# Dependencies written by hand, another end of the program and another column order in a decoder layer on eight cores

## The reference

```
h  = rms_norm(x, g_pre_mix);  q, k, v, u, gates = split(h @ w_in)
q, k = rope(q), rope(k)                     # 12 heads of 64
for (window, dilation) in ((128,1), (512,4), (2048,16)):   # 4 heads each
    out_g, lse_g = causal window attention on keys t - i*dilation
o_attn = sum_g softmax_g(lse_g) * out_g     # 256 wide
y_pool = multi-scale trailing means of u, mixed per group, scaled
merged = sigmoid(gate_a) * (o_attn @ w_proj_attn) + sigmoid(gate_p) * (y_pool @ w_proj_pool)
x  = x + rms_norm(merged @ w_out, g_post_mix)
h2 = rms_norm(x, g_pre_ffn);  a, b = split(h2 @ w_gate_up)   # 2 x 2816
x  = x + rms_norm((silu(a) * b) @ w_down, g_post_ffn)
```

## Time and profile before

| | |
|---|---|
| median of three runs | 993.15 us (993.02 to 994.73) |
| span of the profiled execution, slowest core | 993.0 us; the cores lie between 989.5 and 993.0 |
| busy: PE / DVE / ACT / POOL | 929.5 / 380.8 / 345.8 / 364.8 us |
| the chain that ended last | PE 79%, ACT 5%, POOL 5%, DVE 5%, issue 4%, DMA 1% |
| DMA moved | 105.03 MB, mean 106 GB/s |

### The profile page before, as it was taken

The page is one execution under the profiler, slowest core; times in us unless marked ns, Lnnn a source line. Parts: engine busy times, 40 slices in busy tenths (PEclk is TensorE's granted clock), DMA queues, the critical chain, the costliest instruction groups (busy, mean ns, idle before and its releaser), DMA issues.

```text
span 993.0 us, 15345 instructions; the slowest of 8 cores (989.5 to 993.0 us)
## 1 busy us (share of the span) xinstructions
PE 929.5 (94%) x5574; PEld 474.3 (48%) x5574; DVE 380.8 (38%) x509; ACT 345.8 (35%) x556; POOL 364.8 (37%) x366
## 2 busy tenths in 40 slices
PE   4989998979989999999889999999999999999992
PEld 2456776545554444444444444444444444444441
DVE  5768645677586334334453122111112111221111
ACT  4697446644446224224773111110101111111110
POOL 1528734646576435336882101102331000001322
PEclk9999999999999999999999999999999999999997
DMA  8968801310244334323876576662324444421221
GB/s 231 289 181 242 171 23 44 48 39 1 44 86 86 64 64 128 64 43 105 270 243 166 108 127 119 114 107 64 127 85 128 85 68 81 80 48 36 93 85 42
DMA packets 30778, 105.03 MB, mean 106 GB/s; under 512 B 3952, under 2 KB 3952, under 8 KB 30704
## 3 DMA queue, kind: packets, MB, share of 16 engines
q0 software_dynamic: 14432, 45.65, 27.2%
q1 hardware_dynamic: 15984, 58.33, 17.3%
q10 hardware_dynamic: 288, 0.06, 0.0%
HBM read 132.90 MB, written 16.78 MB: 151 GB/s over the span
## 4 chain that ended last, share of the span: by engine, by line
PE 79%; ACT 5%; POOL 5%; DVE 5%; issue 4%; DMA 1%; POOLq 0%; ACTq 0%; DVEq 0%; SPq 0%
PE ps L637 70%; PE ps L635 10%; DVE PT_75_117 L635 1%; ACT PT_75_117 L635 1%; DMA xst_37_79<-xo 1%; ACT xsb_53_95 L635 1%; POOL x1b_101_143 L635 1%; POOL x1b_102_144 L635 1%; ACT acc_70 L635 1%; POOL x1b_104_146 L635 1%; ACT junk_54_96 L635 1%; POOL x1b_103_145 L635 1%; ACT xsb_52_94 L635 0%; DVE PT_74_116 L635 0%; ACT junk_55_97 L635 0%
## 5 line engine op out<-in xcount | busy, mean ns | idle before, releaser
L637 PE MATMUL ps<-wdna_155,ffT_154 128*128 128x512 bf16 x512 | 115.7, 379 | 0.0
L637 PE MATMUL ps<-hT_68,wgu_109_151 128*128 128x512 bf16 x420 | 100.4, 379 | 0.0
L637 PE MATMUL ps<-hT_68,wgu_110_152 128*128 128x512 bf16 x420 | 100.4, 379 | 0.0
L637 PE MATMUL ps<-hT_68,wgu_111_153 128*128 128x512 bf16 x392 | 93.7, 379 | 0.0
L637 PEld LDWEIGHTS ps<-wdna_155,ffT_154 128*128 128x128 bf16 x512 | 50.1, 98 | 60.4
L637 PEld LDWEIGHTS ps<-hT_68,wgu_109_151 128*128 128x128 bf16 x420 | 41.0, 98 | 49.3
L637 PEld LDWEIGHTS ps<-hT_68,wgu_110_152 128*128 128x128 bf16 x420 | 41.0, 98 | 49.1
L637 PEld LDWEIGHTS ps<-hT_68,wgu_111_153 128*128 128x128 bf16 x392 | 38.3, 98 | 46.3
L637 PE MATMUL ps<-hT_68,wgs_76_118 128*128 128x512 bf16 x224 | 53.6, 379 | 0.6 <-ACT tg_80_122 L635 0.6
L637 PE MATMUL ps<-hT_68,wgs_77_119 128*128 128x512 bf16 x224 | 53.6, 379 | 0.0
L635 DVE TENSOR_TENSOR ffT_154<-ps,sa_115_157 128x512 bf16<-128x512 f32 x30 | 20.7, 691 | 79.2 <-PE ps L635 79.2
(11 more groups left out here) (499 smaller groups left out, 1821.2 us busy)
## 6 DMA issues: line engine op xcount, KB each, us to landing
wgu_109_151<-wgu POOLq DMA_DIRECT2D x15, 512.0 KB, 5.7
wgu_110_152<-wgu POOLq DMA_DIRECT2D x15, 512.0 KB, 5.7
wgu_111_153<-wgu POOLq DMA_DIRECT2D x14, 512.0 KB, 5.6
wgs_76_118<-wg POOLq DMA_DIRECT2D x8, 512.0 KB, 5.5
wgs_77_119<-wg POOLq DMA_DIRECT2D x8, 512.0 KB, 5.2
wdna_155<-wdn POOLq DMA_DIRECT2D x8, 512.0 KB, 8.4
tab_70_112<-tab SPq DMA_DIRECT2D x6, 512.0 KB, 6.0
tab_71_113<-tab SPq DMA_DIRECT2D x6, 512.0 KB, 7.3
```

What stands on the lines that cost most here:

```text
L637: e.ops.append(lambda q, m=method, a=a, k=k: getattr(q, m)(*a, **k))
```

## The change

Six things change.

1. The automatic dependencies (`touch`, `where`, `move_in`) go. Each call names the nodes after which it runs (`after`), each tile names the nodes that give it back (`free`), and a ring that lies over older buffers names the nodes that it must follow (`follow`). Keys, values and queries of groups 1 and 2, `oT2` and `yp` become rings; their slots are claimed by the matmuls.
2. The planner's costs change.
3. `finish` makes only SyncE wait, for all outputs.
4. In `down`, tiles 8 to 15 take Sqrt and reciprocal instead of GpSimd's power; the residual of all tiles is added on VectorE; the last tile is done in two halves of 512 columns.
5. Queries of groups 1 and 2 stand in the order (rho, m, a), token = 16a + 4m + rho, and so do `acc`, the masks and the view of the product into `oT2`. Group 1 then takes its queries and writes its results in 16 runs of 8 columns or more, where there were 4 runs of 32 or more.
6. The first norm's Sqrt takes scale 1 and bias D*EPS (its gain is multiplied by 32), and a dummy Sqrt stands at the start of ScalarE.

```diff
     def finish(self, last):
-        need = {}
+        e, need = self.sp, {}
         for n in last:
             need[n.tick[0]] = max(need.get(n.tick[0], 0), n.tick[1])
-        for e in self.engs:
-            for p, v in need.items():
-                if e.seen.get(p, 0) < v:
+        for p, v in need.items():
+            if e.seen.get(p, 0) < v:
...
-    P.run(out_evs[-4:])
+    P.run(out_evs)
```

```diff
 def op_cost(eng, method, aps, kw):
     if eng == "tensor":
         if method == "transpose":
-            return 0.115
+            return 0.06
-        return max(n * (0.00024 if rows <= 32 else 0.000422), 0.03)
+        return 0.013 + 0.00025 * n if rows <= 32 else max(n * 0.000422, 0.03)
...
-        return 0.12 + (0.00170 if strided else 0.00110) * n
+        return 0.12 + 0.00110 * n
-    return 0.17 + (0.0040 if strided else 0.0021) * n
+    return 0.17 + (0.0040 if strided else 0.0021 if unit_step(peek(aps[0])) else 0.0025) * n
```

```diff
+    m_warm = dve.memset(warm_t[:, :], 1.0)
+    act.activation(out=warm_t[:, 1:2], in_=warm_t[:, 0:1], func=AF.Sqrt, after=[m_warm])
...
-            act.activation(out=s_[:, 0:1], in_=s_[:, 0:1], func=AF.Sqrt, scale=1.0 / D, bias=EPS)
+            e = act.activation(out=s_[:, 0:1], in_=s_[:, 0:1], func=AF.Sqrt, scale=1.0, bias=D * EPS, after=[sq])
```

```diff
-                    act.activation(out=acc[:, :, h, :].rearrange("p s (rho a m) -> p m rho s a", rho=4, m=4)[:, r4],
+                    c = act.activation(out=acc[:, :, h, :].rearrange("p s (rho m a) -> p m rho s a", rho=4, m=4)[:, r4],
...
         def q0f(i, w):
-            return lambda half, h: fap(qs[HR(h), 0, half, 32 * i:32 * i + 32], [(128, 4), (1, 32 * w)])
+            return lambda half, h: fap(qs[HR(h), 0, half, 8 * i:512], [(32, 16), (1, 8 * w)])
         def o0f(i, w):
-            return lambda bk: fap(bk[:, 32 * i:32 * i + 32], [(128, 4), (1, 32 * w)])
+            return lambda bk: fap(bk[:, 8 * i:512], [(32, 16), (1, 8 * w)])
```

```diff
     def down(i):
...
-        out_evs.append(norm_add(b, gfin, xi, out_d, r)[1])
+        if i < NT - 1:
+            rs, sq = rstd(y, junkd, ms, by_pool=i < NT // 2)
+            g = dve.tensor_tensor(out=x1[:, :], in0=y, in1=gfin[:, :], op=ALU.mult, after=[sq, v_gfin])
+            w = dve.scalar_tensor_tensor(out=x1[:, :], in0=x1[:, :], scalar=rs[:, 1:2], in1=xi[:, :], op0=ALU.mult, op1=ALU.add, after=[rs.tok, g, xi.tok])
+            out_evs.append(sp.dma(out_d[r, :], x1[:, :], after=[w]))
+            return
+        for h2 in range(2):
+            c = slice(h2 * 512, (h2 + 1) * 512)
+            sq.append(act.activation(out=j[:, c], in_=b[:, h2, :], func=AF.Square, accum_out=s_[h2][:, 0:1], after=[ms[h2]]))
+            g.append(dve.tensor_tensor(out=x1[:, c], in0=b[:, h2, :], in1=gfin[:, c], op=ALU.mult, after=[sq[h2], v_gfin]))
+            if h2 == 0:
+                e = dve.tensor_scalar(out=s_[0][:, 1:2], in0=s_[0][:, 0:1], scalar1=D * EPS, scalar2=None, op0=ALU.add, after=[sq[0]])
+        q = act.activation(out=s_[1][:, 0:1], in_=s_[1][:, 0:1], func=AF.Sqrt, scale=1.0, bias=s_[0][:, 1:2], after=[sq[1], e])
+        p = dve.reciprocal(out=s_[1][:, 1:2], in_=s_[1][:, 0:1], after=[q])
+        for h2 in (1, 0):
+            w.append(dve.scalar_tensor_tensor(out=x1[:, c], in0=x1[:, c], scalar=s_[1][:, 1:2], in1=xi[:, c], op0=ALU.mult, op1=ALU.add, after=[p, g[h2], xi.tok]))
+            out_evs.append(sp.dma(out_d[r, c], x1[:, c], dsem("d_out%d" % h2), after=[w[-1]]))
```

```diff
-        with pe.group():
+        with pe.group([cp, d_ident]) as tr:
             for k in range(8):
                 pe.transpose(out=psb[:, k, :], in_=xb[:, k * 128:(k + 1) * 128], identity=ident[:, :])
-        dve.tensor_tensor(out=dst, in0=psb, in1=gain.unsqueeze(2).to_broadcast([128, 8, 128]), op=ALU.mult)
+        xb.free(tr)
+        h = dve.tensor_tensor(out=dst, in0=psb, in1=gain.unsqueeze(2).to_broadcast([128, 8, 128]), op=ALU.mult, after=[tr, v_gains] + war)
+        b.free(h)
...
-    for k in range(8):
-        pool.dma(wout[:, k, :], wout_d[:, k, :], dsem("d_wo%d" % k))
+    d_wout = [pool.dma(wout[:, k, :], wout_d[:, k, :], dsem("d_wo%d" % k), after=w01_mm) for k in range(8)]
...
+    xin = P.ring("xin", [128, D], F32, [R3 + i * 4 * KB for i in range(4)], follow=att_all)
```

More of the change, by code:

```diff
@@ L145, in call @@
             n = self.prog.node(self)
[L146 to L152, removed]
-        n.items.append((method, args, kw))
[L154 to L164, removed]
+        aps = [a for a in args if isinstance(a, (bass.AP, View))]
+        aps = [kw[k] for k in ("out",) if k in kw] + aps + [a for k, a in kw.items() if k != "out" and isinstance(a, (bass.AP, View))]
+        n.items.append((method, args, kw))
+        n.after.update(a.idx for a in after if a is not None)
+        self.prog.place_of(n, aps)
+        n.cost += op_cost(self.name, method, aps, kw)
+        n.port |= self.name == "vector" and sum(not in_psum(a) and nelem(peek(a)) > 1 for a in aps[1:]) > 1
+        if method == "activation" and TABLES.get(kw["func"]):
+            n.table = TABLES[kw["func"]]
         return n
@@ L175, in dma @@
         n.cost = 0.55 if self.name == "gpsimd" else 0.06
+        n.dst = out if isinstance(out, View) else in_
         n.sem = sem
         n.prio -= ahead
-        self.prog.close(n)
+        if sem is not None:
+            if sem.prior is not None:
+                n.after.add(sem.prior)
+            sem.prior = n.idx
         return n
@@ L419, in close, with place_of @@
-    def close(self, n):
-        self.touch(n)
-        if n.sem is not None:
-            last = getattr(n.sem, "last", None)
-            if last is not None:
-                n.deps.add(last)
-            n.sem.last = n.idx
+    def place_of(self, n, aps):
+        for x in aps:
+            if isinstance(x, View) and x.tile not in n.tiles:
+                n.tiles.append(x.tile)
+                n.after.update(x.tile.ring.follow)
     LAT = 0.1
@@ L670, in run @@
     def run(self, last):
+        for v in self.tiles:
+            assert v.left, ("never given back", v.ring.views[0].tensor.name, v.seq)
         self.schedule()
@@ L888, in mm8 @@
-    def mm8(out, lhs, rhs, nk=8, claim=(), after=()):
-        with pe.group(claim) as n:
+        xb.free(tr)
+        h = dve.tensor_tensor(out=dst, in0=psb, in1=gain.unsqueeze(2).to_broadcast([128, 8, 128]), op=ALU.mult, after=[tr, v_gains] + war)
+        b.free(h)
+        return cp, h
+    def mm8(out, lhs, rhs, nk=8, after=(), claim=()):
+        with pe.group(after) as n:
+            for t in claim:
+                n.tiles.append(t)
+                n.after.update(t.ring.follow)
             for k in range(nk):
-                pe.matmul(out, lhs(k), rhs(k), start=(k == 0), stop=(k == nk - 1), after=after)
+                pe.matmul(out, lhs(k), rhs(k), start=(k == 0), stop=(k == nk - 1))
@@ L1007, in att_qk @@
+    both0 = masks[:, 0, 128:384]
+    def att_qk(pair, items, mask, after):
         pt, sb = PT.new(), sc2.new()
-        with pe.group():
+        with pe.group(after) as m:
             for kf, qf, c0, n in items:
@@ L1021, in v_lhs, with att_pv @@
         return vb[:, o_:o_ + 2, :]
[L1023 to L1025 removed]
+    def att_pv(pair, ob, pt, items, first, after):
+        with pe.group([pt.tok] + after) as m:
             for hh in range(2):
```

798 lines of the change are left out of this document (417 added, 381 removed).

## The result

The changed kernel takes 988.16 us (median of 4 runs, 986.66 to 990.25) against 993.87 us before (993.02 to 994.73): a ratio of 0.9942, 95% interval 0.9926 to 0.9959. It is faster, but by 5.7 us where 14.5 were forecast, and outside the range of 970 to 987.5. The profiled execution took 990.25 us with a span of 988.6; its slowest core is core 4, where it was core 3 before.

What follows compares the result with a forecast made beforehand. TensorE was taken as the bound, full from 530 us on, with 17.8 us idle at the end. 993.0 - 8.4 - 3.3 - 2.5 - 0.3 = 978.5, with 0.15 added 978.6 us; range 970 to 987.5.

Steps and rivals of the forecast that it cites:

- What bounds the kernel: Whole kernel: TensorE is the bound, full from 530 us on; its longest idle stretch is 17.8 us behind the last matmul.
- parts 1 and 2: Kernel's end: GpSimd's drain moves beside TensorE work, gain 8.4 us; last tile in halves, gain 3.3 us (2.7 to 3.9).
- Part 3: Attention, group 3's sums: contiguous copies from PSUM into acc near 600 instead of 1127 ns; gain 2.5 us (0 to 4.25).
- the oT product: GpSimd in 200:340: writing every 16th bfloat16 instead of every 4th costs 0 to 8 x 0.75 us; taken as 0.
- The short runs: Group 1's queries and results on TensorE in runs of 8 or 16 columns: cost taken as 0, 13.1 us at half rate.
- rival (d): Group 1's attention: short runs slow TensorE, slower than before from a factor of 2.1, 998.3 us at 2.5; chance 4%.
- Part 4: Start of ScalarE: a dummy Sqrt loads the table while the first tile is on its way; gain 0.3 us (0 to 1.3).
- Part 5: 20:340 and 455:530: hand-placed waits and other planner costs change the order; taken as 0, 7 us either way.
- (b): New order worse by some 7 us, as a TensorE queue held by a slot claim: 985 to 990 us; chance 11%.
- My own check: Last matmul: if it moves by more than 7 us either way, the order, not the priced terms, decided.

Runs made afterwards that it cites:

- all_wait: The changed kernel with the old `finish`, in which every engine waits for the outputs: 996.2 us, 8.1 us more than the change.
- tracked kernel: The kernel before with the changed end, column order and planner costs, its automatic dependencies kept: 976.4 us, ratio 0.9818 to the kernel before.
- wout_early: The changed kernel with the loads of wout, gpost and gfin no longer waiting for the last pooled block's matmuls: 984.9 us, ratio 0.9907 to the kernel before.
- both_halves: The changed kernel with the second half of each rotation's matmuls waiting for the same key slot as the first half: 991.7 and 992.3 us.
- tail_only: The kernel before with the changed `finish` and `down` alone, the order before the tail kept: 981.8 us, ratio 0.9875 to the kernel before.

## Why the prediction was wrong, step by step

- **What bounds the kernel, and the tail (parts 1 and 2): right.** Forecast 11.7 us, measured 12.4 on the old order. The drain is 8.4 us, as read from the earlier trace rows, and 8.1 in the times of all_wait; the rest, 4.0 to 4.3, lies just beyond the upper of the two bounds for the last tile (2.7 to 3.9).
- **Part 3, the contiguous copies: right in mechanism, mis-sized.** The copies went from 1127 to 594 ns as read from the earlier trace rows. I took 2.5 us with 4.25 as the upper bound, TensorE's idle time in 140:200; measured were 7.7. The stretch itself gave 4.3, all of its idle time. Most of the rest, 3.1, came at 240 to 260 us, where one wait of TensorE got shorter and the low clock behind it went; I had looked for nothing behind 200 us, and that it helped and didn't hurt is luck. I gave the oT product nothing; it costs 1.1 us each, and what that costs the whole is not shown.
- **The short runs, and rival (d): cost nothing.** The changed kernel's timeline, answering, has 0.34 us from the first of seven query matmuls to the one behind them, as before, and 0.32 for three result matmuls:

```profile
205.45 0.60 PE L501 MATMUL ps<-q,k 32*128 32x256 bf16 x7
205.79 0.27 PE L499 MATMUL ps<-q,k 32*128 32x256 bf16 x1
210.56 0.49 PE L501 MATMUL ps<-PT,v 128*128 128x256 bf16 x3
210.88 0.27 PE L499 MATMUL ps<-PT,v 128*128 128x256 bf16 x1
```

  The pieces are 16 columns long in these rows; result matmuls of 128 columns, in pieces of 8, start 0.056 us apart before and after. The rule of the Trainium skill's "PSUM — Partial Sum Buffer", section Specifications, that a non-contiguous pattern slows matmuls significantly, does not show in them.
- **Part 4, the table load: wrong in sign.** 0.3 us forecast as a gain, with nothing as the lower bound; 1.4 us lost, through the other plan, as far as can be told.
- **Part 5, the order: the step that failed.** I wrote that each new list "names work that is done before the data is wanted", and gave it 0 with 7 us either way. The order, the table load's 1.4 included, costs 13.6. The reasoning asked of each list whether its work ends before the data is read. It did not ask what the waiting instruction holds meanwhile, nor what the list leaves unguarded: half a projection ran ahead and kept two PSUM banks (9.6 us in the tracked kernel, where it could be tried alone). For wout the sentence was not even true: its first matmul comes at 414.0 us instead of 387.3. The kernel before has TensorE at work for all 115.00 us of 340:455, the change for 108.3 besides its fillers, and wout_early gives back some 3 of that.
- **The rivals.** (b), a TensorE queue held by a slot claim at 985 to 990 us, had 11% and is what happened in time and, in part, in kind: what held TensorE's queue was not the slot claim itself but the banks that it left taken. That its price was nearly twice the 7 us it named was hidden by part 3, which gave 5 us more than forecast. My own check stands: the last matmul moved by more than 7 us, so the order decided.
- **What stays open.** The split costs 9.6 us in the tracked kernel, and mending it there gives everything back. For the changed kernel that is not shown: mending it alone costs 3.5 to 4.1 us more (both_halves), mending it beside wout's 3.3 gives 1.1 to 1.6, and one instruction more can move the plan by as much (1.4). 983.3 is still 7 us above 976.4, and more than half of that lies ahead of 200 us: without fillers 94 to 96 and 58.5 us of work in 20:140 and 140:200, against 96 to 99 and 60.0. The late fillers are excluded; which of the other lists (value slots, group 3's results waiting for all value blocks, the pooled branch's waits) keep it was not separated. Nor do the costs of waits simply add: on the tracked order wout's wait was free.

## What to carry to other kernels

Price a new order by asking, for each wait, what the waiting instruction and its partners already hold: a unit that shares a buffer waits as a whole or not at all (in the tracked kernel that gave everything back, in the changed one it did not). Time each part on the old order first; here two parts gave 19.6 us, and the rest of the same change took 13.6 of it away. A stage's idle time bounds what that stage can give (4.3 against 4.25 us here), not what the edit gives: look at what meets differently behind it. And compare stages by real work, with the fillers taken off and on a core whose trace is whole.

## What the runs showed of the hardware that was not expected

GpSimd's closing DRAIN takes 8.4 us when it begins after everything else (8396 ns in two kernels) and 9.3 us when it begins beside other work (9282 ns, at 885.5 in the change and at 878.5 in tail_only). A GpSimd product that writes every 16th bfloat16 instead of every 4th takes 2.43 us instead of 1.35.
